# A two-layer decoder trunk on eight cores: MLP weights shared by two blocks, x in HBM between sub-layers, and weight casts with padded rows

## What is computed

```python
for i in range(2):
    h = rmsnorm(x, g_pre_mix[i])
    if i == 0:                          # 6 retention heads of 128, 128-token chunks
        q, k, v, gate, mq = split(h @ w_in_ret)
        self_out = groupnorm(retention_chunkwise(rotary(q), rotary(k), v)) * silu(gate)
    else:                               # 12 causal heads of 64 with forget gates
        q, k, v, f_logit, mq = split(h @ w_in_fox)
        self_out = forgetting_attention(q, k, v, log_sigmoid(f_logit + b_forget))
    mem_out = memory_attention(mq, mem, g_mem[i], w_mem_kv[i])   # 4 heads, 256 memory tokens
    x = x + rmsnorm(concat(self_out, mem_out) @ w_out[i], g_post_mix[i])
    h = rmsnorm(x, g_pre_mlp[i])
    u = relu(h @ w_up[i])               # 1024 -> 4096
    x = x + rmsnorm((u * u) @ w_down[i], g_post_mlp[i])          # 4096 -> 1024
return x
```

## Time and profile before

| what | value |
|---|---|
| median of 3 runs | 4070.56 us (4067.52 to 4134.98) |
| the profiled execution's own time | 4051.66 us |
| its span, slowest core (core 0) | 4050.0 us |
| other cores | 4028.7 to 4047.4 us |
| PE busy over the span | 3335.4 us (82%) |
| DVE, ACT, POOL busy | 48%, 43%, 9% |
| DMA | 593.78 MB, 147 GB/s |

### The profile page before, as it was taken

The page is one execution under the profiler, slowest core; times in us unless marked ns, Lnnn a source line. Parts: engine busy times, 40 slices in busy tenths (PEclk is TensorE's granted clock), DMA queues, the critical chain, the costliest instruction groups (busy, mean ns, idle before and its releaser), DMA issues.

```text
span 4050.0 us, 55575 instructions; the slowest of 8 cores (4028.7 to 4050.0 us)
## 1 busy us (share of the span) xinstructions
PE 3335.4 (82%) x16157; PEld 1519.7 (38%) x16476; DVE 1935.6 (48%) x3309; ACT 1728.1 (43%) x3117; POOL 346.8 (9%) x314
## 2 busy tenths in 40 slices
PE   2003147899999999999998899999998999999997
PEld 0001013444444444444443444444433444444443
DVE  2002057544645675534426666465456665444252
ACT  1001134334463344375584444353734443664841
POOL 0000000000000121101001221000001220010010
PEclk8556569999999999999999999999999999999999
DMA  9999952444446555443535545444465454435334
GB/s 146 122 127 132 125 132 93 158 141 140 154 141 188 181 163 178 147 143 122 156 105 174 174 155 177 146 148 145 146 183 169 152 168 156 145 124 159 105 115 130
DMA packets 198261, 593.78 MB, mean 147 GB/s; under 512 B 49024, under 2 KB 60928, under 8 KB 196224
## 3 DMA queue, kind: packets, MB, share of 16 engines
q1 hardware_dynamic: 195296, 538.03, 41.6%
q0 software_dynamic: 2672, 52.17, 11.0%
HBM read 605.48 MB, written 88.87 MB: 171 GB/s over the span
## 4 chain that ended last, share of the span: by engine, by line
PE 64%; DMA 9%; DVE 8%; another core or an unknown queue 7%; issue 5%; ACT 4%; POOL 1%; SPq 1%; DVEq 0%; ACTq 0%; POOLq 0%
PE pb L599 64%; DVE un_s L619 2%; DMA wm_s<-wbf 2%; DMA xt_s<-xT 2%; DMA vcache<-un_s 2%; DVE tb_s L622 1%; DMA rot<-xt_s 1%; ACT rs_s L610 1%; ACT sq_s L610 1%; DMA wf_s<-wbf 1%; DVE hb_s L622 1%; DVE hb_s L631 1%; ACT rb_s L610 1%; ACT un_s L610 1%
## 5 line engine op out<-in xcount | busy, mean ns | idle before, releaser
L599 PE MATMUL pb<-u_s,wf_s 128*128 128x512 bf16 x4006 | 969.6, 381 | 40.3 <-ACT sq_s L610 28.3
L599 PE MATMUL pb<-hb_s,wf_s 128*128 128x512 bf16 x3995 | 946.2, 383 | 47.7 <-DMA wf_s<-wbf 13.8
L599 PE MATMUL pb<-hb_s,wm_s 128*128 128x512 bf16 (+1 forms) x2178 | 595.3, 391 | 135.2 <-DMA wm_s<-wbf 102.9
L599 PEld LDWEIGHTS pb<-hb_s,wf_s 128*128 128x128 bf16 x4096 | 394.8, 98 | 523.1 <-issue 87.6
L599 PEld LDWEIGHTS pb<-u_s,wf_s 128*128 128x128 bf16 x4096 | 396.3, 98 | 490.0 <-issue 53.6
L610 ACT ACTIVATE pt_s<-pb,dcol_s 128x512 bf16<-128x512 f32 x960 | 535.3, 627 | 71.9 <-PE pb L599 65.5
L610 ACT ACTIVATE rb_s<-pb 128x512 bf16<-128x512 f32 x512 | 304.2, 595 | 470.7 <-PE pb L599 373.7
L599 PE MATMUL pb<-un_s 65*128 65x512 bf16 (+5 forms) x1536 | 410.1, 307 | 70.3 <-DVE rs_s L619 62.6
L619 DVE TENSOR_TENSOR u_s<-rb_s 128x512 bf16<-128x512 bf16 x512 | 254.0, 496 | 445.8 <-ACT rb_s L610 444.0
L610 ACT ACTIVATE sq_s<-pb 128x512 bf16<-128x512 f32 x304 | 180.9, 596 | 637.3 <-DVE hb_s L631 613.7
L631 DVE CAST hb_s<-pb 128x512 bf16<-128x512 f32 x256 | 176.6, 690 | 390.7 <-PE pb L599 389.7
(11 more groups left out here) (67 smaller groups left out, 2445.4 us busy)
## 6 DMA issues: line engine op xcount, KB each, us to landing
wf_s<-wbf SPq DMA_DIRECT2D x512, 512.0 KB, 3.7
wm_s<-wbf SPq DMA_DIRECT2D x152, 768.0 KB, 4.7
xt_s<-xT SPq DMA_DIRECT2D x176, 256.0 KB, 6.8
wbf<-wall POOLq DMA_DIRECT2D x32, 1024.0 KB, 19.9
wm_s<-wbf SPq DMA_DIRECT2D x32, 512.0 KB, 4.1
outT<-xt_s SPq DMA_DIRECT2D x64, 256.0 KB, 2.7
wbf<-wall POOLq DMA_DIRECT2D x19, 768.0 KB, 14.8
vcache<-un_s SPq DMA_DIRECT2D x64, 144.0 KB, 4.4
```

The lines of the kernel that those rows point to most:

```text
L599: S.add("pe", lambda e: e.matmul(out, lhsT=lhsT, rhs=rhs, start=start, stop=stop, **kw), reads=reads, writes=writes, cost=c)
```

## The change

Stages now go layer by layer: all four blocks of a sequence through layer 0, then all four through layer 1. The MLP takes two blocks at once except for the first two blocks of the first sequence in layer 0. A pair goes through the 4096 in two halves, so that `u2` holds half for each block: up half, down half with the partial sums stored to HBM (`y1`), up of the other half, down of it with the partial sums read back and added. x is stored to HBM (`xs`) and read again at every seam, and only one seam is open at a time; `xB` shrinks to 14 tiles, `hb` grows from three to four blocks. The rows of `wall` are padded from 1024 to 1040 values, so that a cast reads rows of 1024 with gaps, and casts no longer wait for one another: the planner spaces them by its own model, with three in flight there. `spare` is gone, and what it chose for goes to POOL always. The mixers' arithmetic and the number of matmuls stay the same. The diff, cut:

```diff
-NXT = 18
-NCAST = 2
+NXT = 14
+WPAD = 16
+NCAST = 3
...
-    return np.concatenate(parts).astype(np.float32), idx
+    wall = np.zeros((n * 128, 1024 + WPAD), np.float32)
+    wall[:, 0:1024] = np.concatenate(parts).reshape(n * 128, 1024)
+    return wall, idx
...
+    xs_d = nc.dram_tensor("xs", [n_seq, NCH, 128, SEQ], F32, kind="Internal").ap()
+    y1_d = nc.dram_tensor("y1", [2, NCH, 128, BLK], F32, kind="Internal").ap()
...
-    for i in range(0, len(items), 2):
-        for l in layers:
-            for s, b in items[i:i + 2]:
-                stages.append((s, l, b))
+    stages = [(s, l, b) for s in range(n_seq) for l in layers for b in range(NBLK)]
...
-            after = [rs_[i - NCAST]] if i >= NCAST else [X[items[0]]["x"][4].R]
+            after = [] if i else [X[items[0]]["x0"][4].R]
+            if i >= NCAST:
+                p_ = rs_[i - NCAST]
+                yield lambda: S.avail["pe"] >= p_.last_w.end - 3000.0
...
-            ...(rows(DR["wbf"], o, n), rows(DR["wall"], o, n)),
+            ...(rows(DR["wbf"], o, n), DR["wall"][o * 128:(o + n) * 128, 0:1024]),
...
     def seam(s, l, gi, b, hb, sm, nl, ngi):
-        xs = X[(s, b)]["x"]
+        yield lambda: not seam_["busy"]
+        seam_["busy"] = True
+        xs = []
+        K.spawn(xload(s, l, gi, b, xs), 1)
...
-            tt(xs[c].ap, xs[c].ap, t.ap, ALU.add, ..., eng=(spare(s, b) if c % 2 else "dve"))
+            tt(xs[c].ap, xs[c].ap, t.ap, ALU.add, ..., eng=("pool" if c % 2 else "dve"))
...
+            K.spawn(xstore(s, b, c, xs[c], nl is None), 0)
...
+    def y_load(ys):
+        for oc in range(NCH):
+            for t in range(2):
+                yield lambda: len(ys) < 4
+                x = yield from xB.acq()
+                yield ("sp", [y1R[t][oc]], [x.R])
+                spdma(x.ap, DR["y1"][t, oc], [y1R[t][oc]], [x.R], x.R, 262144)
+                ys.append(x)
+
+    def y_part(t, oc, bk):
+        x = yield from xB.acq()
+        if t:
+            yield ("dve", [bk.R], [x.R])
+            cp(x.ap, bk.ap, [bk.R], [x.R])
+        else:
+            yield ("act", [bk.R], [x.R])
+            act(x.ap, bk.ap, AF.Copy, [bk.R], [x.R])
+        bk.busy = False
+        yield ("sp", [x.R], [y1R[t][oc]])
+        spdma(DR["y1"][t, oc], x.ap, [x.R], [y1R[t][oc]], x.R, 262144)
+        x.busy = False
+
+    def y_whole(s, l, hb, oc, bk, sm, x):
+        yield ("dve", [bk.R, x.R], [x.R])
+        tt(x.ap, bk.ap, x.ap, ALU.add, [bk.R, x.R], [x.R])
+        bk.busy = False
+        sq = yield from sqB.acq()
+        yield ("act", [x.R], [sq.R])
+        act(sq.ap, x.ap, AF.Square, [x.R], [sq.R])
+        K.spawn(sq_into(sm, sq), 0)
+        e_ = "pool"
+        yield (e_, [x.R], [hb.R[oc]])
+        cp(hb.ap[:, oc, :], x.ap, [x.R], [hb.R[oc]], eng=e_)
+        x.busy = False
+        sm.y += 1
...
+                for bl in ([(0,), (1,)] if first else [(0, 1)]) + [(2, 3)]:
+                    yield from mlp_job(s, l, bl)
...
+        nh = len(bl)
+        nf = 32 // nh
+        for half in range(nh):
+            for f in range(nf):
+                if f % 2 == 0:
+                    key = ("up", l, (half * nf + f) // 2)
+                    wu, wR, _ = yield from WF.take(key)
+                for t, hb in enumerate(hbs):
+                    ...                      # 8 matmuls up, ReLU, square into u2[nf * t + f]
+            if half:
+                K.spawn(y_load(ys), 1)
+            for oc in range(NCH):
+                ...                          # one load of down weights, 16 matmuls for each block
+                    elif half:
+                        yield lambda: ys
+                        K.spawn(y_whole(s, l, hb, oc, bk, sms[t], ys.pop(0)), 0)
+                    else:
+                        K.spawn(y_part(t, oc, bk), 0)
```

More of the change, by code:

```diff
@@ L463, in schedule @@
     u2R = [Res(f"u2_{f}") for f in range(32)]
+    xsR = [[[Res(f"xs{s}_{b}_{c}") for c in range(NCH)] for b in range(NBLK)] for s in range(n_seq)]
+    y1R = [[Res(f"y1_{t}_{c}") for c in range(NCH)] for t in range(2)]
+    seam_ = {"busy": False}
     mkvB = Bufs(tiles("mkv", 2))
@@ L776, in seam, with xstore, xload @@
             yield from normed(s, nl, ngi, b, xs, sm2, hb)
-    def xload(s, b, xs):
+        seam_["busy"] = False
+    def xstore(s, b, c, t, last):
+        yield ("sp", [t.R], [])
+        spdma(DR["out" if last else "xs"][s][c, :, bsl(b)], t.ap, [t.R], [] if last else [xsR[s][b][c]], t.R, 262144, final=last)
+        if last:
+            t.busy = False
+    def xload(s, l, gi, b, xs):
+        src, r_ = (DR["xT"], None) if l == layers[0] and gi < 2 else (DR["xs"], xsR[s][b])
         for c in range(NCH):
             t = yield from xB.acq()
-            yield ("sp", [], [t.R])
-            spdma(t.ap, DR["xT"][s][c, :, bsl(b)], [], [t.R], t.R, 262144)
+            rd = [r_[c]] if r_ else []
+            yield ("sp", rd, [t.R])
+            spdma(t.ap, src[s][c, :, bsl(b)], rd, [t.R], t.R, 262144)
             xs.append(t)
@@ L791, in first_norm @@
         if i == 0:
[L792 removed]
+            yield from xload(s, layers[0], 0, b, xs)
             for t in xs:
                 K.spawn(square(sm, t.ap, t.R), 0)
[L795 removed]
+            X[(s, b)]["x0"] = xs
             K.spawn(caster(), 0)
@@ L1451, in mixer @@
             K.spawn(mem_attn(s, l, b), 3)
-            if i % 4 in (0, 3) and items.index((s, b)) + 1 < len(items):
-                K.spawn(ahead(i, s, b), 1)
+            if i + 1 < len(stages) and stages[i + 1][1] == layers[0]:
+                K.spawn(ahead(s, l, b, stages[i + 1]), 1)
             if ret:
@@ new lines, in y_whole @@
+    def y_whole(s, l, hb, oc, bk, sm, x):
[6 more added lines that the diff above has]
+        K.spawn(sq_into(sm, sq), 0)
+        e_ = "pool"
+        yield (e_, [x.R], [hb.R[oc]])
+        cp(hb.ap[:, oc, :], x.ap, [x.R], [hb.R[oc]], eng=e_)
+        x.busy = False
+        sm.y += 1
+    def mlp():
+        for s in range(n_seq):
+            for l in layers:
+                first = s == 0 and l == layers[0]
+                for bl in ([(0,), (1,)] if first else [(0, 1)]) + [(2, 3)]:
+                    yield from mlp_job(s, l, bl)
@@ L1516, in schedule, with mlp_end @@
+    def mlp_end(s, l, b, hb, sm, nl):
+        yield lambda: sm.y == NCH
+        yield from seam(s, l, 3, b, hb, sm, nl, 0)
     K.spawn(first_norm(0), 1)
```

123 lines of the change are left out of this document (58 added, 65 removed).

## The result

| | before | after |
|---|---|---|
| median of 4 runs | 4072.53 us (4067.52 to 4134.98) | 3880.38 us (3874.03 to 3927.74) |
| span of the profiled execution | 4050.0 us | 3879.1 us |
| PE busy | 82% | 86% |
| DMA | 593.78 MB | 637.95 MB |

The ratio is 0.9557 (0.9464 to 0.9651): faster, but by about half of what was forecast.

What follows compares the result with a forecast made beforehand. The prediction saw a start bound by DMA, where casts delay loads, then a rest bound by PE. Steady pace 3552, minus 22 catching-up, plus 162 start loss and 10 tail gave 3702 us span, about 3720 measured; range 3620 to 3850.

Steps and rivals of the forecast that it cites:

- DMA in the start: Start: casts and loads summed on the DMA engines, layer 0's last weight at 467 us; start loses 162, not 498.
- The allowance for layer 1's casts: Start, after layer 0's last weight: 218 us of casts and 262 of loads nearly fit under PE work; 50 us allowed.
- The loss of the first stage: Start, until layer 0's last weight: 467 us pass for 355 us of PE work at the steady pace, 112 us lost.
- The landing time of 5 us: Mixer weight loads in the start: 768 KB lands in about 5 us instead of 40, each row waiting 0.28 us.
- The stage order: Start: layer 1 is wanted only after four blocks of layer 0, so 102 of 199 units are urgent.
- The pairs: MLP in pairs with partial sums: weight loads fall from 512 to 288; taken at nothing, ends -40 and +60 us.
- The price of a cast row: Casts in the start: a padded row costs 0.281 us of an engine, all 25,472 rows 448 us.
- Unchained casts behind POOL's additions: POOL in the start: casts issue without waits but in program order with additions that may wait; taken at nothing.
- The padding does not shorten q0's turn: Rival, 6%: many short cast rows go in one turn, loads still land in 40 us; about 4057 us, no change.
- SP's queue stalls: Rival, 5%, slower: 304 added stores wait in SP's in-order queue, holding weight loads; full 2.8 us each gives 4570 us.
- The DMA competition hides too: Rival, 16%: POOL's additions hold layer 1's casts back until PE has its loads; start loss 70 us, time 3627 us.
- The rest pays: Rival, 9%: partial sums hold a bank while additions wait for loads; steady PE share 90%, 160 us more, 3880 us.

Runs made afterwards that it cites:

- e7: The kernel before with only the gap behind each row of 1024 values added, casts still chained: ratio 0.9531, span 3868.5 us.
- e6: The changed kernel without padding and with POOL's early additions and products on DVE, so all casts are issued at once: span 4067.4 us, ratio not given.
- e10: The changed kernel with POOL's early additions and products on DVE and a gap every 4096 values instead of every 1024: ratio 0.9954, span 4035.9 us.
- e5: The changed kernel, padding kept, with POOL's early additions and products on DVE, so they do not pace the casts: ratio 0.9676, span 3944.5 us.
- e2: The changed kernel without the padding, each cast one contiguous run again: ratio 0.965, span 3888.2 us.
- e9: The changed kernel without layer 1's casts, its weights loaded from layer 0's units: span 3732.2 us, ratio not given.
- e13: The changed kernel casting only the 38 units of layer 0's mixers, which serve for all weights: ratio 0.9056, span 3666.7 us.
- e4: The changed kernel with single-block MLP jobs and the old order of stages: ratio 0.9652, span 3906.2 us.
- e3: The changed kernel with every MLP taken one block at a time, no pairs or partial sums: ratio 0.9789, span 3966.9 us.
- e11: The changed kernel with each cast waiting on the chip for the one two before it: ratio 0.9486, span 3850.4 us.

## Why the prediction was wrong

*The direction was right, and so was the mechanism of the turns*: long casts kept loads waiting, and shorter turns let them through (e7; e6, e10, e5 as a series). That this kernel owes its gain to the padding was not right: without it e2 gains 132 of the 148 us in the start, because POOL's additions pace the casts, a term that I took at nothing. *The size was wrong*: a start gain of 498 - 162 + 22 = 358 us was forecast, and 148 came; the rest gave 23 where the tail was to cost 10. 210 - 33 = 177 us, the whole difference between 3702 and 3879.

**The step that failed: "DMA in the start".** It added up megabytes as if the engines worked on what was needed first, and let layer 1's casts fill gaps for an allowance of 50 us. Nothing does that ordering. At 467 us, when the step had the last layer-0 weight arrive with 72 MB of loads and 336 us of PE work, the trace of after shows:

```profile
0.00:467.00 467.00, 236.47 (x1052) 103.94 (x1071) 191.55 (x362) 138.80 (x259) 78.15 (x95) 0.77 0.97 170
```

```profile
q0 software_dynamic: 16722, 33.01, 59.2%
q1 hardware_dynamic: 18284, 46.25, 37.5%
```

The casts are ahead of the plan (33.01 MB, where layer 0's 102 units are 26.7) and the loads behind it (46.25 of 72 MB). 1052 matmuls at 0.205 us are 216 us of work instead of 336. In terms of the sum:

- The allowance for layer 1's casts, 50 us (0 to 100), was really 308 - 148 = 160 us (e9 against after, in the start). Even the upper end was too low, because I bounded it by how full the engines had to be and not by who would be served. This is 110 of the 210 us.
- The loss of the first stage, 112 us, was some 100 larger: without layer 1's casts the start gains 308 us, where the sum without the allowance had 408. Loads beside casts run at 272 MB/ms, not at the 324 that I took from the time after the casts: 72 MB take 265 us, not 224, an estimate of 41 us. Layer 0's MLP casts cost 80 us in the start (e13); how much of that is loads served late rather than the DMA work itself was not separated, so some 60 us stay without a single cause. The clock, which the sum left out, may be part of them: in the first 400 us of e9, at a granted clock of 0.79 and 0.76, PE takes 199 us for 894 matmuls, an estimated 16 us more than at the 0.205 us of the rest.

The landing time of 5 us (8 rows, each behind one cast row) failed in the same way: it counted the casts' rows alone in front of a load. With both queues full a load also stands behind what SP has issued before it, which I take to be the missing time; no run separated it. Measured were 22.5 us, and the marks "under 15 us" and "mixer 1 before 200 us" (264) both missed.

*Two terms that failed and nearly cancel.* The stage order was to leave only 102 of 199 units urgent. By itself it gains next to nothing in the start (162 us in e4, 169 in e3) and costs 61 us of span. The pairs were taken at nothing, 40 us at best; in that order they save 88.

*Right terms.* The price of a cast row, taken from the same operation: 26,221 packets in 0.580 x 735 us of all engines, 0.26 us where I had 0.281; in all 427 us (11.0% of 3879) against 448, a little under the mark of 440 to 510. The traffic of x and partial sums is hidden in the rest, with pairs: 44 MB more in all, 95.7% PE, loads in 4.0 and 5.2 us. The tail: 35 us from the last MLP matmul (3844.0) to the end, forecast 32. DMA over 85% busy past 600 us: yes.

*Unchained casts behind POOL's additions.* I costed this at nothing. POOL's order is a pacing, and makes e2 work; giving up the chain may have cost up to the 29 us of e11.

*The rivals.* "The padding does not shorten q0's turn" fell: in e7 a mixer load lands in 14.8 us instead of 40.2, and in e6 one row of q1 goes between two of q0. The rule of the Trainium skill, "DMA: Bandwidth & Descriptors", section "Queues, rings and completion order", that a queue keeps its turn for a packet, typically 9 to 17 descriptors, is not what these two queues do in e6, where 97% of q1's rows are followed at once by a packet of q0. "SP's queue stalls" fell: SP waits longer for POOL, and PE does not notice. "The DMA competition hides too" fell furthest; its opposite happened. "The rest pays" gave 3880 us, the number that was measured, by a mechanism that did not occur: PE's share rose to 95.7%. That agreement is chance, and it shows why a time alone proves no theory.

## What to carry to other kernels

When two queues compete and both are full, sum what each gets by the alternation (row against row, by their lengths), not by what the program needs first: an early transfer that is not urgent takes as much as an urgent one. So hold unurgent bulk work back in the issuing program; here this was worth 76 us with not a byte less moved. And try the smallest part alone: padding each cast row on the old kernel gave the whole gain, and the pairs only earned back most of what the rest of the change cost.

## What the runs showed of the hardware

- The turn between q0 (issued by POOL) and q1 (issued by SP) is one row each: 2147 packets to 2081 with both queues full and rows of very different length (e6, 50 to 450 us). In e5 q0 has more, 20,823 to 16,846 in 525 us; I take it that q1 runs empty at times there, which was not measured. Long contiguous casts, back to back, leave q1 11.3% of the engines, and a 768 KB load takes 91.8 us (e6).
- Loads beside casts cost more engine time for each MB than alone: 272 against 327 MB/ms in one and the same kernel (e9). The packets beside the casts are also smaller, 2.50 against 2.86 KB in the mean; whether that is all of it is open.
- To issue a cast takes POOL 0.62 us with some 450 rows in it (26,400 packets in 58 casts) and 0.495 us with 45: a tenfold number of packets costs a quarter more.
- POOL can run only so far ahead with short rows: in e5 it issued 39 casts at once and was then held 4.8 to 19 us before each of the others, by nothing that the profile shows. In e6, with a tenth of the packets, it issued all 58 at once.
- The granted clock (1 is 2.4 GHz, 0.5 is 1.2 GHz) lay between its two levels in the start: 0.76 from 200 to 400 us in e9, where PE did 515 matmuls, 0.89 in e13, where it did 795, and 0.79 from 0 to 200 us in e9, with 379.
